# The skip term of a state-space prompt phase: from VectorE to TensorE and ScalarE

## What is computed

```python
y_diag = jnp.einsum('bgcls,bgjcls,bcsgjp->bclgjp', cb, _seg_decay(a), X)
...
y_off = jnp.einsum('bclgn,bcgjpn,bgjcl->bclgjp', Cc, new_states[:, :-1], jnp.exp(cs))
y = (y_diag + y_off).reshape(Bsz, T, H, P)
...
y, hT = _ssd(xs * dt[..., None], dt * A, Bm, Cm, h0.astype(f32))
y = y + xs * D_skip.astype(f32)[:, None]
```

## Time and profile before

| | us |
|---|---|
| median of 3 runs | 4437.52 (4434.76 to 4447.11) |
| the profiled execution, its own time | 4441.11 |
| its span | 4439.5 |
| TensorE busy | 4170.6 (94%) |
| VectorE busy | 3179.5 (72%) |
| ScalarE busy | 1432.4 (32%) |
| GpSimd busy | 1366.4 (31%) |
| start of the phase's first work, start of the next phase's | 1110.1, 1221.2 |

### The profile page before, as it was taken

The page is one execution under the profiler, slowest core; times in us unless marked ns, Lnnn a source line. Parts: engine busy times, 40 slices in busy tenths (PEclk is TensorE's granted clock), DMA queues, the critical chain, the costliest instruction groups (busy, mean ns, idle before and its releaser), DMA issues. The chain is left out here.

```text
span 4439.5 us, 85485 instructions
## 1 busy us (share of the span) xinstructions
PE 4170.6 (94%) x32575; PEld 3789.2 (85%) x32575; DVE 3179.5 (72%) x6008; ACT 1432.4 (32%) x2183; POOL 1366.4 (31%) x1063
## 2 busy tenths in 40 slices
PE   7999999998768989999999998999999999999997
PEld 4888888887537869878888888999999999999996
DVE  5631343444844248899976665999999999999997
ACT  2221222221654222233346674222222222222223
POOL 6433331000032200054433233433434434434430
PEclk9999999999869999999999999999999999999998
DMA  4665666465533311144435546999999999999994
GB/s 170 201 199 189 205 223 213 180 225 165 155 128 112 123 63 34 51 142 143 142 116 179 208 176 239 318 301 301 301 300 300 304 300 298 303 298 300 303 298 157
DMA packets 523005, 928.00 MB, mean 209 GB/s; under 512 B 284033, under 2 KB 351233, under 8 KB 518689
## 3 DMA queue, kind: packets, MB, share of 16 engines
q1 hardware_dynamic: 387024, 549.29, 38.2%
q0 software_dynamic: 80960, 346.96, 23.3%
q10 hardware_dynamic: 54816, 28.85, 2.2%
HBM read 785.79 MB, written 206.30 MB: 223 GB/s over the span
## 5 line engine op out<-in xcount | busy, mean ns | idle before, releaser
L3298 POOL DMA_INDIRECT ex_rows<-expert_rows,ex_here x512 | 586.7, 1146 | 954.7 <-DVE acc_tok L3433 863.9
L3433 DVE SCALAR_TENSOR_TENSOR acc_tok<-ex_rows,ex_wsp,acc_tok 128x1024 f32<-128x1024 f32 x512 | 634.5, 1281 | 0.2 <-issue 0.2
L2665 PE MATMUL ex_psa<-x_dense_high,eg_u_high 128*128 128x288 f32 x2048 | 605.7, 296 | 11.6 <-ACT ex_w L3361 8.5
L2665 PE MATMUL ex_psa<-x_dense_low,eg_u_high 128*128 128x288 f32 x2048 | 605.7, 296 | 0.0
L2665 PE MATMUL ex_psa<-x_dense_high,eg_u_low 128*128 128x288 f32 x2048 | 605.3, 296 | 0.0
L2756 POOL TENSOR_TENSOR eg_u_low<-eg_u,eg_u_high 128x1024 fp32r<-128x1024 f32 x130 | 335.3, 2580 | 798.3 <-ACT eg_u_high L2751 798.3
L3330 PE MATMUL ex_pso<-ex_w_high,ex_v_high 128*128 128x288 f32 x2048 | 441.4, 297 | 8.9 <-DVE acc L3415 8.9
L3361 ACT ACTIVATE ex_w<-ex_psa 128x288 f32<-128x288 f32 x256 | 105.4, 412 | 1056.1 <-PE ex_psa L2665 1056.1
L3330 PE MATMUL ex_pso<-ex_w_high,ex_v_low 128*128 128x288 f32 x2048 | 440.1, 297 | 0.0
L3330 PE MATMUL ex_pso<-ex_w_low,ex_v_high 128*128 128x288 f32 x2048 | 438.9, 296 | 0.0
L3415 DVE TENSOR_TENSOR acc<-ex_pso,acc 128x576 f32<-128x576 f32 x512 | 374.7, 753 | 47.7 <-PE ex_pso L3330 47.7
(11 more groups left out here) (510 smaller groups left out, 9199.4 us busy)
## 6 DMA issues: line engine op xcount, KB each, us to landing
eg_u<-in_u SPq DMA_DIRECT2D x256, 512.0 KB, 3.6
expert_rows<-in_v SPq DMA_DIRECT2D x128, 512.0 KB, 7.0
ex_v<-in_v SPq DMA_DIRECT2D x128, 512.0 KB
weights<-wt_stage SPq DMA_DIRECT2D x9, 4096.0 KB, 13.0
ex_g<-weights SPq DMA_DIRECT2D x128, 288.0 KB
expert_rows<-eg_act SPq DMA_DIRECT2D x256, 128.0 KB, 1.7
proj<-in_out POOLq DMA_DIRECT2D x50, 548.5 KB, 6.4
in_w<-in_w_in SPq DMA_DIRECT2D x50, 512.0 KB, 4.7
```

The source lines that it names most:

```text
L2665: yield nc.tensor.matmul(out[:, 0:b - a], w[:, kc, :], half[:, kc, a:b], start=n == 0, stop=n == len(passes) - 1)
L3298: pool.indirect_dma_start(rows[i][:, :], None, table, index(here[par][:, t, j:j + 1]), element_offset=ROW_RUNS[t][0]).then_inc(s_row[i], 16)
L3433: v.scalar_tensor_tensor(out=acc_tok[:, t, :], in0=rows[i][:, at:at + D], scalar=wsp[:, i:i + 1], in1=acc_tok[:, t, :], op0=ALU.mult, op1= ...
```

## The change

Seven edits, all in `phase_ssd_prompt` and `load_z`:

1. GpSimd makes, once, eight diagonal matrices 128 x 128, one for each channel tile, with D on the diagonal: the identity times D's column (L1644 of the changed kernel). They lie in tile 7 of `z`, which is otherwise not filled yet.
2. TensorE's `back(c)` opens each pair's sum in PSUM with the product of that diagonal matrix and the chunk's x (L1677), over all 128 partitions; the heads' two products are added to it.
3. VectorE's eight scalar_tensor_tensor of each chunk are gone, and with them its `skip` step.
4. ScalarE copies the finished chunk, 128 x 1024, from PSUM to `ob` (`evacuate`, L1701): chunk c-2 before the exp of chunk c, the last two at the end.
5. TensorE's next `back` waits for that copy as well, since PSUM is written again.
6. SP's load of x for chunk c waits for y of chunk c-3 in place of its skip.
7. SP loads tile 7 of `z` only after the last y, just ahead of the store of the state.

```diff
@@ sync
                     if c >= 3:
-                        sp.wait_ge(DB.sem, DB.done("skip", c - 3))
+                        sp.wait_ge(PB.sem, PB.done("y", c - 3))
...
-                load_z(k, sp, z)
+                load_z(k, sp, z, range(KC - 1))
+                sp.wait_ge(PB.sem, PB.done("y", NSC - 1))
+                load_z(k, sp, z, range(KC - 1, KC))
                 sp.wait_ge(DB.sem, DB.done("s", NSC - 1))
...
+            @block.gpsimd
+            def _(pool):
+                pool.wait_ge(k.s_d, 32)
+                nc.gpsimd.tensor_tensor(diag, bc(k.ident[:, :].unsqueeze(1), [P, KC, P]), bc(d[:, :].unsqueeze(2), [P, KC, P]),
+                                        ALU.mult).then_inc(s_diag, 1)
@@ tensor, back(c)
                     if c:
                         pe.wait_ge(DB.sem, DB.done("s", c - 1))
+                        pe.wait_ge(s_ev, c)
                     else:
                         pe.wait_ge(s_S, 1)
+                        pe.wait_ge(s_diag, 1)
                     pe.wait_ge(DF.sem, DF.done("w", c))
-                    for i in range(SH):
-                        o_ = yv[64 * (i % 2):64 * (i % 2) + 64, i // 2, :]
-                        nc.tensor.matmul(o_, xt[h][:, i, :], w[h][:, i, :], start=True, stop=False)
-                        mm = nc.tensor.matmul(o_, S[:, i, :], ce[h][:, i, :], start=False, stop=True)
+                    for pair in range(KC):
+                        nc.tensor.matmul(yv[:, pair, :], diag[:, pair, :], inx[c % 3][:, pair, :], start=True, stop=False)
+                        for q, part in enumerate(halves()):
+                            i, o_ = 2 * pair + q, yv[part, pair, :]
+                            nc.tensor.matmul(o_, xt[h][:, i, :], w[h][:, i, :], start=False, stop=False)
+                            mm = nc.tensor.matmul(o_, S[:, i, :], ce[h][:, i, :], start=False, stop=True)
@@ scalar
+                def evacuate(c):
+                    act.wait_ge(PB.sem, PB.done("y", c))
+                    a.activation(ob[:, :, tok(c)], yv, ACT.Copy).then_inc(s_ev, 1)
...
                     if c >= 2:
+                        evacuate(c - 2)
                         act.wait_ge(PB.sem, PB.done("s", c - 2))
...
+                evacuate(NSC - 2)
+                evacuate(NSC - 1)
@@ vector, back(c)
                     dve.wait_ge(PB.sem, PB.done("y", c))
-                    for i in range(KC):
-                        last = v.scalar_tensor_tensor(out=ob[:, i, tok(c)], in0=inx[c % 3][:, i, :], scalar=d[:, i:i + 1], in1=yv[:, i, :],
-                                                      op0=ALU.mult, op1=ALU.add)
-                    last.then_inc(*DB.inc("skip"))
                     v.tensor_tensor(S[:, :, :], S[:, :, :], bc(end[h][:, :].unsqueeze(2), [P, SH, SD]), ALU.mult).then_inc(*DB.inc("decay"))
```

More of the change, by code:

```diff
@@ L1610, in phase_ssd_prompt @@
         yv = ps[:, 4:6, :].rearrange("p a b -> p (a b)").rearrange("p (a l) -> p a l", a=KC)
+        diag = z[:, KC - 1, 0:KC * P].rearrange("p (i c) -> p i c", i=KC)
         s_S = k.sem("sp_state_zeroed")
         s_out = k.sem("sp_state_stored")
+        s_diag = k.sem("sp_skip_diagonals_made")
+        s_ev = k.sem("sp_y_evacuated")
         PF = Progress(k.sem("sp_pe_front"), "col", "bc", "x")
@@ L1616, in phase_ssd_prompt @@
         DF = Progress(k.sem("sp_dve_front"), "cb", "x", "xd", "end", "ce", "w")
-        DB = Progress(k.sem("sp_dve_back"), "skip", "decay", "s")
+        DB = Progress(k.sem("sp_dve_back"), "decay", "s")
         tok = lambda c: slice(c * SL, (c + 1) * SL)
@@ L1745, in _ @@
                 dve.wait_ge(s_S, 1)
-                dve.wait_ge(k.s_d, 32)
                 front(0)
@@ L1751, in _, with load_z @@
                     back(c)
-def load_z(k, eng, z):
-    for i in range(KC):
+def load_z(k, eng, z, tiles):
+    for i in tiles:
         (_, zp), (_, zs) = predecessor_views(k.io["proj"][Z0 + i])
```

## The result

The changed kernel takes **4453.81 us** (median of 7 runs, 4448.62 to 4463.97), the kernel before 4439.54 (7 runs beside them, 4434.76 to 4447.11). The ratio is 1.0032, with a 95% interval of 1.0020 to 1.0043, so between 9 and 19 us slower. The forecast was no change, 4439.5, with a range up to 4449; the time lies 4.8 us above that range.

A forecast was written before the change was run, and what follows sets the result against it. VectorE bounds the phase, then TensorE and the loop through ScalarE, both near 12 us a chunk. Terms +0.3, +0.25, -0.4, +1.0 and +1 make +2.1 us; from the median 4437.5 that gives 4439.5 us, no change, range 4425 to 4449.

The forecast's parts named there:

- What bounds the kernel, and who takes over: In the changed phase VectorE, 98% busy, bounds at 12.00 us a chunk; afterwards TensorE and a ScalarE loop, both about 12.
- What leaves VectorE, and the most to be gained: Eight VectorE skip instructions a chunk go, 2.06 us a chunk; at most some 16 us, 0.37% of the kernel, gained.
- The main term, +3.9 us of TensorE time a chunk: Diagonal products and width switches make a pair 0.94 to 0.95 us, a chunk's y products 7.6 in place of 3.70.
- The first period: From chunk 0's first y product to chunk 1's: 13.55 us against 13.26, +0.3, full clock forecast from chunk 1 on.
- rival 3: Later chunks' y partly at half clock: up to 12 us, 4451, chance 0.12; half clock throughout: some +85 us, 0.03.
- y(6) to y(7) and the tail: Last period between chunks' y products, without a front: -0.4 us; last y to the state's store: 11.05 against 10.05, +1.0.
- The store, +1: At the phase's end the late z tile shares engines with the state's store: bounds 0 and 2.8 us, taken as 1.
- The copy, GpSimd's product, the new waits: ScalarE's copy takes 1.1 us a chunk, under its bound; GpSimd's product and TensorE's wait on the copy cost nothing.
- What lies outside the phase: No term: the forecast summed only the changed phase's differences, against the profiled execution of 4441.1 us.
- Rival 1: TensorE's width switch is free: y 5.25 us a chunk, the loop through ScalarE bounds at 10.7, 4427 us; chance 0.18.
- Rival 2: TensorE's addition is hidden altogether and ScalarE's 10.1 us a chunk bounds: -16 us, 4421; chance 0.04.
- Rival 4: A pair's heads on TensorE no longer overlap: pair 1.16 us, y 9.3, period 13.7, +14.5 us, 4452; chance 0.06.

The follow-up runs named there:

- the run with halves: Changed kernel with each 128-column diagonal (skip) product made as two products of 64 columns, in all chunks: median 4431.99 us, ratio 0.9977 to the kernel before.
- wide ones in twos: Changed kernel with the 128-column diagonal products of two pairs in a row, then both pairs' heads: median 4443.04 us, ratio 1.0008 to the kernel before.
- second look: The kernel before, unaltered, profiled once more for comparison: 4447.96 us in one run, phase 112.7 us.
- The two padded runs: 64 one-column VectorE clears added to the changed kernel (1.0017 to the kernel before) and to 64-column halves with ScalarE's exp ahead of its copy (0.9973).

## Why the prediction was wrong

By its own steps:

- **What bounds the kernel, and who takes over.** Right. VectorE at 98% was the bound, and with the skip gone it waits; TensorE was busy for 85.29 of 85.30 us, and the loop through ScalarE lay close behind it, as the run with halves showed.
- **What leaves VectorE, and the most to be gained.** Right: 13.4 us without the diagonal product (97.7 against 111.1), against an upper bound of 16.
- **The main term, +3.9 us of TensorE time a chunk.** The mechanism is right, the size a little small: 8.0 - 3.7 = 4.3. The pair took 1.01 us and not 0.94 to 0.95. The step that was mis-sized is "0.11 between the two records of the diagonal product", taken from a group inside a row of wide products. Right behind a switch the second record starts 0.21 us after the first; the 0.11 holds for the first pair after the front alone, whose neighbour is wide. The two switches, 0.20 each, came out at 0.205 and 0.20. The eight head records took 0.39 and not 0.43, so a pair is 0.21 + 0.205 + 0.39 + 0.20 = 1.01. That makes the five periods +1.57 instead of +0.25.
- **The first period: the failed step.** The prediction took y(0) as "5.25 + 3.9", that is, with the same piece at half clock as before and the rest at full. Measured was 14.26, because the whole of y(0) ran at 0.50, and nearly all of the s products behind it as well (3.26 us in place of 1.90). Against the forecast of 13.55 that is +5.1 for y(0), +1.4 for s and -0.1 for the front: the 19.93 us measured. This is 6.4 of the 7.2 us by which the phase missed its forecast. It is rival 3's mechanism, in chunk 0 alone. Rival 3 asked whether later chunks fall to half clock, because they start after a stop; the row that spoke against it (0.97 in a phase of narrow products) changes its column count 92 times in 7081 records, once in 77, where y(0) of the changed kernel does so 15 times in 80. That the order of widths does it is shown by the runs: wide products one at a time 11.4 to 17.0 us to the rise, halves 2.8 to 4.1, wide ones in twos 5.9, as in the kernel before's second look. Why such an order holds the clock down is not shown.
- **y(6) to y(7) and the tail.** -0.45 against -0.4; +1.46 against +1.0, the excess again from the longer pair.
- **The store, +1.** Zero, here and in the kernel before with the late tile.
- **The copy, GpSimd's product, the new waits.** They cost nothing that shows: the copy lasted 1.02 us (the estimate was 1.1), and the run without the diagonal product has them all and is 13.4 us shorter in the phase.
- **What lies outside the phase.** Left out altogether. The prediction summed the phase, as if the rest were a constant. The top-k phase got 2.6 us longer, by the stalls at its loop's jump. The two padded runs show its cause, the length of VectorE's program. The final phase took 46.5 to 46.7 us in the kernel before, its second look and the run with late z, and 47.0 to 48.9 in all others, padded or not. But the expert phase ahead of it took 1661.4 to 1661.9 us in those three and 1658.3 to 1660.9 in the nine profiles of the changed kernel and its variants. Together the two phases took 1708.1 to 1708.5 us in the three and 1707.8 on average in the nine (1706.4 to 1709.8): no loss of the change shows there.

Together +9.3 and +2.6, that is 11.9 of the 14.3 us between the medians; both are differences of single executions, good to 1 or 2 us, and the interval of the ratio is 9 to 19 us. What remains has no place that the profiles show.

**The rivals.** Rival 1 (the switch is free) is refuted: 0.36 us of a pair's 1.01 go to it. Rival 2 (all hidden, -16 us) needed y at 3.7; it was 8.0. Rival 4 gave 4452 us, near the time that came, and is wrong all the same: the heads still overlap, four records of L1680 together in about 0.4 us, and the period was 12.32, not 13.7. A time that fits is no evidence for a mechanism. Rival 3 was right about the resource and wrong about the place. The rule that products keep program order, which rival 4 took from the Trainium skill, stands in TensorE: Matmul & The Clock Gate under "Step-by-step: what each phase is for", not in the section that rival 4 names; the changed kernel's trace differs from it as the earlier trace rows did, with the four records of L1680 from 1151.98 ahead of those of L1681 from 1152.25.

## What to carry to other kernels

When small products are put between products of another width on TensorE, count the switches and not only the records: here 0.22 us of work brought 0.36 us of switching, and cutting the wide product into two of the neighbours' width turned a loss of 0.3% into a gain of 0.2%, though it doubled the number of products. Cost a stretch's first chunk by itself when it starts at half clock, with the mix of products that it will have. And when an edit changes the length of an engine's program, compare the phases behind it, the jumps of their loops above all: a phase that gained 4.8 us left the kernel's time where it was.

## What the runs showed of the hardware that was not expected

- **The granted clock can stay at 0.50 under a TensorE that never idles.** With wide and narrow products taking turns it was 0.50 through all 14.2 us of y(0) in two executions and for 11.4 us in a third, with TensorE busy for all of it. In the nine other profiles that start y(0) at half clock, with narrow products alone or with the wide ones in twos, it rose after 2.8 to 5.9 us. Once at 1.00 it stayed there through the same alternation.
- **A switch of width costs in both directions, and the first record behind it twice.** At full clock it is 0.20 us each from start to start, in place of 0.055 or 0.11, and then 0.21 in place of 0.11 for the second wide record.
- **A shorter program can be slower.** 64 instructions fewer on VectorE brought stalls of 3.90 and 2.43 us at a jump more than 900 us later, 56 fewer one of 3.38 us at another jump, and with 64 idle clears put back there was none.
